# Memory attention with its operands split in high and low parts: three single-pass matmuls in place of one full-precision matmul

## The reference

```python
def memory_xattn(h, mem_n, w_mem_q, w_mem_kv, w_mem_o):
    B, S, _ = h.shape
    q = (h @ w_mem_q).reshape(B, S, MEM_HEADS, MEM_HEAD_DIM)      # 4 heads of 512
    kv = (mem_n @ w_mem_kv).reshape(B, N_MEM, 2, MEM_HEADS, MEM_HEAD_DIM)
    k, v = kv[:, :, 0], kv[:, :, 1]
    s = jnp.einsum('bqhd,bkhd->bhqk', q, k).astype(jnp.float32) * (MEM_HEAD_DIM ** -0.5)
    p = jax.nn.softmax(s, axis=-1).astype(v.dtype)
    o = jnp.einsum('bhqk,bkhd->bqhd', p, v).reshape(B, S, D_MODEL)
    return o @ w_mem_o
```

## Time and profile before

| | us |
|---|---|
| median of three timed runs | 1808.76 |
| the profiled execution, its own time | 1808.44 |
| its span, from the first to the last instruction | 1806.7 |
| PE matmul busy | 1795.1 (99% of the span) |
| PE weight loads busy | 1501.0 (83%) |
| DVE busy | 1058.4 (59%) |
| ACT busy | 922.0 (51%) |
| POOL busy | 60.7 (3%) |

### The profile page before, as it was taken

One profiled execution on the slowest core, in us unless ns is written; L12 is line 12 of the kernel. 1 busy time (PEld: TensorE's weight loads), 2 busy tenths in 40 slices (PEclk: granted clock), 3 DMA queues, 4 the chain that ended last, 5 costly groups with the idle time before them and its releaser, 6 DMA issues.

```text
span 1806.7 us, 25113 instructions
## 1 busy us (share of the span) xinstructions
PE 1795.1 (99%) x8736; PEld 1501.0 (83%) x8736; DVE 1058.4 (59%) x1503; ACT 922.0 (51%) x1270; POOL 60.7 (3%) x132
## 2 busy tenths in 40 slices
PE   9999999999999999999999999999999999999998
PEld 7888888888887888888888878888888888888886
DVE  5554555555555554544444477777777777844444
ACT  7555566665545554544544474444444444443443
POOL 4000000000000110000000100000000000000000
PEclk9999999999999999999999999999999999999999
DMA  8455554455556565555444556555555555665553
GB/s 285 151 187 178 173 162 148 155 161 165 189 205 233 189 189 182 182 173 191 152 139 149 198 168 224 188 188 187 187 186 186 186 186 180 244 209 187 184 189 111
DMA packets 166408, 330.69 MB, mean 183 GB/s; under 512 B 7846, under 2 KB 13398, under 8 KB 164950
## 3 DMA queue, kind: packets, MB, share of 16 engines
q1 hardware_dynamic: 164806, 318.48, 53.5%
q10 hardware_dynamic: 1552, 11.54, 1.6%
HBM read 325.81 MB, written 4.19 MB: 183 GB/s over the span
## 4 chain that ended last, share of the span: by engine, by line
PE 98%; DVE 1%; ACT 0%; DMA 0%; issue 0%; SPq 0%; DVEq 0%; ACTq 0%
PE bank L462 22%; PE bank L464 22%; PE bank L463 22%; PE bank L868 17%; PE bank L870 9%; PE bank L494 1%; PE bank L778 1%; PE bank L795 1%; PE bank L660 1%; PE bank L661 1%; DMA bufX<-in_x 0%; PE bank L677 0%; PE bank L668 0%; DVE actA L1692 0%; PE bank L569 0%
## 5 line engine op out<-in xcount | busy, mean ns | idle before, releaser
L1392 DVE TENSOR_TENSOR wlo<-raw,whi 128x1024 fp32r<-128x1024 f32 x612 | 746.9, 1222 | 694.7 <-ACT whi L971 517.2
L971 ACT ACTIVATE whi<-raw 128x1024 fp32r<-128x1024 f32 x448 | 471.5, 1052 | 582.9 <-PE bank L464 373.2
L868 PE MATMUL bank<-actA,whi 128*128 128x512 f32 x1344 | 472.0, 394 | 0.0
L870 PE MATMUL bank<-actA,wlo 128*128 128x256 f32 x1344 | 380.2, 283 | 0.0
L868 PEld LDWEIGHTS bank<-actA,whi 128*128 128x128 f32 x1344 | 252.5, 188 | 58.1
L462 PE MATMUL bank<-whi,actA 128*128 128x512 f32 x672 | 274.7, 409 | 1.3 <-DVE wlo L1392 0.5
L464 PE MATMUL bank<-whi,actA 128*128 128x512 f32 x672 | 265.3, 395 | 0.0
L463 PE MATMUL bank<-wlo,actA 128*128 128x512 f32 x672 | 265.0, 394 | 0.0
L957 ACT ACTIVATE whi<-raw 128x1024 fp32r<-128x1024 f32 (+1 forms) x164 | 168.7, 1032 | 171.2 <-PE bank L464 156.9
L870 PEld LDWEIGHTS bank<-actA,wlo 128*128 128x128 f32 x1344 | 252.8, 188 | 0.0
L462 PE MATMUL bank<-whi,actB 128*128 128x512 f32 x576 | 229.5, 398 | 0.0
(11 more groups left out here) (230 smaller groups left out, 1460.6 us busy)
## 6 DMA issues: line engine op xcount, KB each, us to landing
raw<-in_w_ffn_in SPq DMA_DIRECT2D x88, 1024.0 KB
raw<-in_w_in SPq DMA_DIRECT2D x48, 1024.0 KB
raw<-in_w_mem_kv SPq DMA_DIRECT2D x32, 1024.0 KB
raw<-in_w_ffn_out SPq DMA_DIRECT2D x32, 1024.0 KB
raw<-in_w_attn_br SPq DMA_DIRECT2D x16, 1024.0 KB
raw<-in_w_mix_out SPq DMA_DIRECT2D x16, 1024.0 KB
raw<-in_w_mem_q SPq DMA_DIRECT2D x16, 1024.0 KB
raw<-in_w_mem_o SPq DMA_DIRECT2D x16, 1024.0 KB
```

Source lines behind the costliest of these rows:

```text
L868: pe.matmul(dst[:, :], whi[:, s, o:o + P], actA[:, :, kt, :], start=(kt == 0), stop=False)
L870: mm = pe.matmul(dst[:, 0:S], wlo[:, s, o:o + P], actA[:, 0, kt, :], start=False, stop=(kt == KD - 1))
L971: act.activation(whi[:, ks % AHEAD, 0:w], raw[:, c, ks % 2, 0:w], ACT.Copy).then_inc(hi_done, 1)
L1392: dve.tensor_tensor(wlo[:, vs % AHEAD, 0:w], raw[:, c, vs % 2, 0:w], f32(whi[:, vs % AHEAD, 0:w]), ALU.subtract).then_inc(lo_done, 1)
```

## The change

The memory attention's two products are now done with three single-pass matmuls each, as the large products are. The queries (`mqr`) and probabilities (`mpr`) are split where ACT copied them before: ACT writes the high part, then DVE subtracts it from the same PSUM tile for the low part, and now it is DVE that raises `at_out` and `mpT_out`. Keys and values are split into one pair of buffers `kvh` and `kvl`, which both take in turn. The keys of the next head are split in k = 7 (those of head 0 by `first_keys`), the values of the head in k = 3 on ACT and in k = 4 on DVE. POOL's copy of the values is gone. The buffers `mqr`, `mpr` and `mp_sb` share the place of `bufY`, and the queries before their transposition stand in `kch`.

```diff
+    heads = ExitStack()
+    mqr = sb(heads, "mqr", [P, 2, 4, S], F32R)
+    mpr = sb(heads, "mpr", [P, 2, 2, S], F32R)
+    mp_sb = sb(heads, "mp_sb", [P, TT, S])
+    heads.close()
     bufY = sb(mixmem, "bufY", [P, TT, D])
...
+    kvh = sb(memp, "kvh", [P, 4 * S], F32R)
+    kvl = sb(memp, "kvl", [P, 4 * S], F32R)
...
-        with pool.Fori(0, ND) as i:
-            pool.wait_ge(acc_out[0], U_MQ + 1 + i)
-            pool.wait_ge(acc_out[1], U_MQ + 1 + i)
-            pool.tensor_copy(mv_sb, memv[:, :, bass.ds(i * NC, NC)]).then_inc(mv_ok, 1)
...
@@ PE
                 if k == 1:
                     pe.wait_ge(at_out, A_MQ + 2 * n + 2)
+                    pe.wait_ge(kv_lo, 2 * n + 1)
                     for t in range(TT):
+                        dst = sc[0][:, t * S:(t + 1) * S]
                         for d in range(4):
-                            mm = pe.matmul(sc[0][:, t * S:(t + 1) * S], mqT[:, d, t * P:(t + 1) * P],
-                                           memk[:, 4 * n + d, :], start=(d == 0), stop=(d == 3))
+                            qh, ql = (mqr[:, h, d, t * P:(t + 1) * P] for h in range(2))
+                            pe.matmul(dst, qh, mk_hi[:, d, :], start=(d == 0), stop=False)
+                            pe.matmul(dst, qh, mk_lo[:, d, :], start=False, stop=False)
+                            mm = pe.matmul(dst, ql, mk_hi[:, d, :], start=False, stop=(d == 3))
...
                 if k in (5, 6):
                     pe.wait_ge(mpT_out, n + 1)
-                    pe.wait_ge(mv_ok, n + 1)
+                    pe.wait_ge(kv_lo, 2 * n + 2)
                     t_wait(T_MOUT + 2 * n + k - 5)
                     for j in range(2):
                         d = 2 * (k - 5) + j
+                        dst = tr[(k - 5) % 2][:, j * S:(j + 1) * S]
                         for b in range(2):
-                            mm = pe.matmul(tr[(k - 5) % 2][:, j * S:(j + 1) * S], mv_sb[:, b, d * P:(d + 1) * P],
-                                           mpT[:, b, :], start=(b == 0), stop=(b == 1))
+                            vh, vl = (v[:, b, d * P:(d + 1) * P] for v in (mv_hi, mv_lo))
+                            pe.matmul(dst, vh, mpr[:, 0, b, :], start=(b == 0), stop=False)
+                            pe.matmul(dst, vl, mpr[:, 0, b, :], start=False, stop=False)
+                            mm = pe.matmul(dst, vh, mpr[:, 1, b, :], start=False, stop=(b == 1))
...
@@ ACT
                 if k == 0:
                     for b in range(2):
-                        at_copy(A_MQ + 2 * n + b, A_MQ + b, mqT[:, 2 * b:2 * b + 2, :].rearrange("p k s -> p (k s)"))
+                        act.wait_ge(at_filled, A_MQ + 2 * n + b + 1)
+                        act.activation(mqr[:, 0, 2 * b:2 * b + 2, :].rearrange("p k s -> p (k s)"),
+                                       at[(A_MQ + b) % 2][:, :], ACT.Copy).then_inc(mq_hi, 1)
...
-                    act.activation(mpT, sc[1][:, :].rearrange("p (b s) -> p b s", b=2), ACT.Copy).then_inc(mpT_out, 1)
+                    act.activation(mpr[:, 0, :, :], sc[1][:, :].rearrange("p (b s) -> p b s", b=2),
+                                   ACT.Copy).then_inc(mpT_hi, 1)
+                if k == 3:
+                    act.activation(mv_hi, memv[:, :, bass.ds(n * NC, NC)], ACT.Copy).then_inc(kv_hi, 1)
...
+                if k == 7 and not (isinstance(n, int) and n == ND - 1):
+                    act.activation(mk_hi, memk[:, bass.ds(4 * n + 4, 4), :], ACT.Copy).then_inc(kv_hi, 1)
...
+        def first_keys(k):
+            if k == 7:
+                act.activation(mk_hi, memk[:, 0:4, :], ACT.Copy).then_inc(kv_hi, 1)
...
@@ DVE
+                if k == 0:
+                    for b in range(2):
+                        dve.wait_ge(mq_hi, 2 * n + b + 1)
+                        hi_, lo_ = (mqr[:, h, 2 * b:2 * b + 2, :].rearrange("p k s -> p (k s)") for h in range(2))
+                        dve.tensor_tensor(lo_, at[(A_MQ + b) % 2][:, :], f32(hi_), ALU.subtract).then_inc(at_out, 1)
...
+                if k == 4:
+                    dve.wait_ge(kv_hi, 2 * n + 2)
+                    dve.tensor_tensor(mv_lo, memv[:, :, bass.ds(n * NC, NC)], f32(mv_hi),
+                                      ALU.subtract).then_inc(kv_lo, 1)
+                    dve.wait_ge(mpT_hi, n + 1)
+                    dve.tensor_tensor(mpr[:, 1, :, :], sc[1][:, :].rearrange("p (b s) -> p b s", b=2),
+                                      f32(mpr[:, 0, :, :]), ALU.subtract).then_inc(mpT_out, 1)
...
+                if k == 7 and not (isinstance(n, int) and n == ND - 1):
+                    dve.wait_ge(kv_hi, 2 * n + 3)
+                    dve.tensor_tensor(mk_lo, memk[:, bass.ds(4 * n + 4, 4), :], f32(mk_hi),
+                                      ALU.subtract).then_inc(kv_lo, 1)
...
```

More of the change, by code:

```diff
@@ L218, in hybrid_layer @@
     rdiag = cu[:, 1, :].rearrange("p (t s) -> p t s", t=TT)
[L219 to L223, removed]
+    mq_sb = kch[:, :, :]
+    mk_hi, mk_lo = (t[:, :].rearrange("p (d s) -> p d s", s=S) for t in (kvh, kvl))
+    mv_hi, mv_lo = (t[:, :].rearrange("p (b n) -> p b n", n=NC) for t in (kvh, kvl))
     psum = ctx.enter_context(nc.psum_tensor("bank", [P, 8, 512], F32))
@@ L255, in hybrid_layer @@
     y_gained, res_done = sem("y_gained"), sem("res_done")
-    mv_ok, m_filled, m_max, m_nmax, m_exp, m_rsum, m_norm = (sem(n) for n in (
-        "mv_ok", "m_filled", "m_max", "m_nmax", "m_exp", "m_rsum", "m_norm"))
-    mpT_filled, mpT_out = sem("mpT_filled"), sem("mpT_out")
+    m_filled, m_max, m_nmax, m_exp, m_rsum, m_norm = (sem(n) for n in (
+        "m_filled", "m_max", "m_nmax", "m_exp", "m_rsum", "m_norm"))
+    mpT_filled, mpT_hi, mpT_out = sem("mpT_filled"), sem("mpT_hi"), sem("mpT_out")
+    mq_hi, kv_hi, kv_lo = sem("mq_hi"), sem("kv_hi"), sem("kv_lo")
     spill, x3_in, stored = sem("spill"), sem("x3_in"), sem("stored")
@@ L1245, in job @@
                             [actB[:, 0, 4 * n + 2 * (k - 5) + j, :] for j in range(2)])
-            return job
+                if k == 7 and not (isinstance(n, int) and n == ND - 1):
+                    act.activation(mk_hi, memk[:, bass.ds(4 * n + 4, 4), :], ACT.Copy).then_inc(kv_hi, 1)
+            return job
+        def first_keys(k):
+            if k == 7:
+                act.activation(mk_hi, memk[:, 0:4, :], ACT.Copy).then_inc(kv_hi, 1)
         mq_t = [mq_sb[:, t, :] for t in range(TT)]
-        column(V_MQ, U_MQ, 0, mq_t, N_X2, nothing)
+        column(V_MQ, U_MQ, 0, mq_t, N_X2, first_keys)
         with act.Fori(1, ND) as n:
@@ L1256, in last_head @@
                 mem_head(ND - 1)(6)
-                act.wait_ge(mv_ok, ND)
+                act.wait_ge(kv_lo, 2 * ND)
                 act.dma_start(gpost, a["g_mem_post"].broadcast_to([P, D])).then_inc(gpost_in, 16)
@@ L1657, in job, with first_keys @@
                                           ALU.mult).then_inc(m_norm, 1)
+                if k == 4:
[5 more added lines that the diff above has]
+                                      f32(mpr[:, 0, :, :]), ALU.subtract).then_inc(mpT_out, 1)
                 if k in (5, 6):
                     t_split(T_MOUT + 2 * n + k - 5, k - 5, *tiles(actB, 4 * n + 2 * (k - 5)))
-            return job
-        column(V_MQ, 0, nothing)
+                if k == 7 and not (isinstance(n, int) and n == ND - 1):
+                    dve.wait_ge(kv_hi, 2 * n + 3)
+                    dve.tensor_tensor(mk_lo, memk[:, bass.ds(4 * n + 4, 4), :], f32(mk_hi),
+                                      ALU.subtract).then_inc(kv_lo, 1)
+            return job
+        def first_keys(k):
+            if k == 7:
+                dve.wait_ge(kv_hi, 1)
+                dve.tensor_tensor(mk_lo, memk[:, 0:4, :], f32(mk_hi), ALU.subtract).then_inc(kv_lo, 1)
+        column(V_MQ, 0, first_keys)
         with dve.Fori(1, ND) as n:
```

## The result

The changed kernel takes 1814.12 us (median of 8 runs, 1813.88 to 1815.85), beside 1808.76 us for the kernel before. The ratio is 1.003, with a 95% interval of 1.002 to 1.0039. The forecast was 1813.4 us, and slower. This is a small effect, 5.4 us or 0.3%, but the interval of the ratio is clear of 1. The profiled execution has a span of 1812.7 us against 1806.7, at the same mean clock of 0.999.

The account below looks back on a forecast made before the run. PE, busy for 99% of the span, was taken as the bound. Waits of 9.5 us less 4.9 saved gave +4.6 on 1808.4, so 1813.1, plus 0.3 for the median: 1813.4 us; range 1811 to 1815.5, widened to 1809.5 to 1816.5.

Parts of the forecast that it names:

- cheaper matmuls, 8 groups: Memory attention's products on PE: eight calls fall from 3.45 to 2.84 us, 4.9 us saved over 8 groups.
- queries, heads 0 to 2: First score matmul: PE waits for DVE's low parts of the queries, 1.35 us a head, 4.05 us for three.
- probabilities, heads 0 to 2: k = 4 and 5: PE waits for DVE's low part of the probabilities, 1.20 us a head, 3.6 for three.
- queries, head 3: Scores of head 3, without a table load: PE starts at 961.87 instead of 961.58, 0.29 us.
- probabilities, head 3: Value product of head 3: PE starts at 977.89 instead of 976.63, 1.26 us.
- unit 6 of head 3: Unit 6 waits for the split output of the first four value calls: 0.39 us instead of 0.08, 0.31 more.
- The two chains: Queries and probabilities through ACT and DVE to PE: DVE ends at 871.15 and 886.05, PE starts at 871.31 and 886.21.
- What was to cost nothing: Stopping POOL's copies, the `kv_lo` wait, and DVE's k = 4 work ahead of a `wlo` over 5 us from use.
- the saving alone remains: Rival: DVE's work between k = 0 and 1 and in k = 4 is covered, giving 1803.9 us; chance 0.07.
- only one chain is late: Rival: ACT's new instruction does not push the k = 0 `whi`, 1810.5 us, or queries never wait, 1809.1; chance 0.15.
- The clock: Rival: PE's waits drop the unit behind each to 1.2 GHz, +19 us, 1833; chance 0.04.
- The weight loads: Rival: PE's 24 loads per eight calls do not overlap, taking 4.1 us instead of 2.84, 1823.7 us; chance 0.02.

Follow-up runs that it names:

- each reordering: Changed kernel with DVE's k = 4 job ahead of its `wlo`: 1809.51 us; or k = 0 query splits ahead of ACT's `whi` and DVE's `wlo`: 1809.45 us.
- The run with the keys in k = 6: Changed kernel with the next head's keys split at the end of k = 6 instead of k = 7: 1811.86 us, ratio 1.0018.
- the version with both reorderings: Changed kernel with k = 0 query splits ahead of `whi` and `wlo`, and DVE's k = 4 job ahead of `wlo`: 1805.23 us, ratio 0.9981.
- the run with the values' low part twice: Changed kernel with DVE writing the values' low part once more, unread, ahead of the true one in k = 4: 1821.95 us, ratio 1.0072.
- The version with two passes: Kernel with both reorderings, less the third matmul of each of the 64 calls, so the output lacks terms: 1797.68 us, ratio 0.9942.

## Why the prediction was right, point by point

| term | predicted, us | in the trace after, us |
|---|---|---|
| cheaper matmuls, 8 groups | -4.9 | -4.6 (8 x (3.45 - 2.88)) |
| queries, heads 0 to 2 | +4.05 (1.35 each) | +4.2 (1.40 in head 0) |
| probabilities, heads 0 to 2 | +3.6 (1.20 each) | +3.5 (1.18 in head 0) |
| queries, head 3 | +0.29 | +0.28 |
| probabilities, head 3 | +1.26 | +1.25 |
| unit 6 of head 3 | +0.31 | +0.29 |
| sum | +4.6 | +5.0 |

The two waits of heads 0 to 2 are counted from head 0. Heads 1 and 2 agree: the three passes take 31.94 (898.61 - 866.67), 31.91 and 31.93 us instead of 30.55, 30.54 and 30.54. That is 1.4 more, where the prediction said 1.3. For head 3 the rows are these, with PE's transposes at 962.45 and 977.62 as anchors:

```profile
966.28 0.39 PE L783 MATMUL bank<-kvh,mqr 128*128 128x256 f32 x1
...
966.50 0.28 PE L784 MATMUL bank<-kvl,mqr 128*128 128x256 f32 x1
...
981.99 0.39 PE L803 MATMUL bank<-mpr,kvh 128*128 128x256 f32 x1 [0.99 <-DVE mpr L1688]
982.22 0.28 PE L804 MATMUL bank<-mpr,kvl 128*128 128x256 f32 x1
...
985.23 0.50 PE L464 MATMUL bank<-whi,actB 128*128 128x512 f32 x1
...
985.57 0.39 PE L465 MATMUL bank<-wlo,actB 128*128 128x512 f32 x1
```

The scores start in effect at 966.50 - 0.12 = 966.38, needed at 962.45 + 3.65 = 966.10 (957.93 to 961.58 in the trace before). The values start in effect at 982.10, needed at 977.62 + 3.23 = 980.85. Unit 6 starts in effect at 985.57 - 0.23 = 985.34, and the 24 matmuls from 982.10 end at 984.97, so it waits 0.37 in place of 0.08.

- **The saving** was right in kind and 0.3 us too large: the price here is 0.120 us a matmul, in the trace and by the passes with 16 matmuls fewer, where the pooling product had 0.1185. The estimate by the Trainium skill ("TensorE: Matmul & The Clock Gate", section "Back-to-back issue gap"), 109 ns, is not borne out by either number. The section gives this gap for a matmul by itself, and says that in a stream with a weight load for each it under-counts at small widths, which the prediction left out. The difference seen here has that direction.
- **The two chains** came out link by link. With the 0.37 us taken off by which this trace starts later, the `whi` of k = 0 ends at 868.67 (predicted 868.69), its `wlo` at 869.94 (869.95), the second low part of the queries at 871.13 (871.15), and PE starts at 871.36 (871.31). The handover from DVE to PE, taken as 0.16 us, was 0.23 here and 0.16 at the probabilities. The experiments show the chains to be causes: each reordering takes away its own waits, together they turn the slower kernel into a faster one, and one more subtraction lengthens each wait by what it adds to DVE's chain, 1.13 us.
- **ACT's keys**, 0.96 us in front of the table load, were a term of the queries' chain. The run with the keys in k = 6 shows it on head 1: 0.18 us of idle time for 1.14.
- **What was to cost nothing** cost nothing. No new wait for `wlo` or `kv_lo` is in PE's list, and neither does delaying `whi` and `wlo` by a job make one in the memory part. The list of the version with both reorderings has one more wait for `wlo`, of 0.2 us, but it lies ahead of 860 us, and the run with the values' low part twice, which is not reordered, has one there too.
- **The rivals.** That the saving alone remains was wrong for this order of DVE's work, and right for another: 1805.23. That only one chain is late is out, as both reorderings gain the same, and so is that ACT's keys do not push the `whi`, by the run with the keys in k = 6. The clock did not fall in the changed kernel's trace. It fell behind two of four waits of nearly twice the length. The weight loads do not bind: a load's row lasts 0.19 us, and the matmuls follow each other every 0.120.
- **What is left over.** In the memory part lie 219.5 - 214.7 = 4.8 us, close to the predicted 4.6. The span has 6.0 more and the medians 5.4. Of the rest about 0.4 is the start of the program. Another 0.8 lies at the very end, where the last outputs are stored: from the start of DVE's last piece in the chain to the end of the span it is 3.1 us in the trace before and 3.9 in the one after. The version with two passes has 3.0 us there, the one with both reorderings 3.9. Why it takes one or the other was not tried. The prediction had a term for neither, so that the total came out within 0.7 us says less for it than the memory part does.

## What to carry to other kernels

Where one engine is busy for 99% of the span, price a cheaper instruction on it together with the latest operand it will then wait for, and follow that operand back through every queue it stands in. Operand chains with little slack belong ahead of work that has a lot: here `whi` and `wlo` are written over 5 us before their use and stood ahead of operands needed at once, and moving three jobs by one place each turned 0.3% slower into 0.2% faster. A side engine's busy share says nothing on this, since DVE was at 59 or 60% in every version.

## What the runs showed of the hardware

- TensorE's granted clock stayed at 2.4 GHz through repeated waits of about 1.2 to 1.4 us, and also through four waits of about 1.8 us. Behind waits of about 2.3 us (idle gaps of 2.07 and 2.10 us in PE's records) it went to 1.2 GHz soon after PE had started again, and back to 2.4 GHz while PE was busy. That trace has two such dips for four waits. Such a wait cost 1.5 us more than itself, and the four runs of that version spread by 3.4 us.
- Single-pass matmuls of 256 columns with a weight load of 0.19 us each follow each other every 0.120 us here, and every 0.1185 in the pooling product. So the loads overlap one another and the matmuls, also where two loads in a row bring the same operand.
- A full-precision call of 256 columns takes 0.43 us, and three single passes 0.36. So splitting saves 17% of such a product on PE (2.88 us for 3.45).
